# Normalizing the attention probabilities of the second block on GpSimd instead of VectorE

## The chip, the cores and the metric

The kernel runs as one program on 1 core of a Trainium2 chip. TensorE multiplies matrices, VectorE and ScalarE do elementwise work, GpSimd elementwise work from SBUF alone, and SyncE issues most of the loads. The metric is the time of one execution on the device in microseconds (us). Before the change the median of 3 runs is 4014.93 us (4013.55 to 4018.3).

## The reference, cut to what matters

Two blocks of two layers each run one after the other on a sequence of 1024 tokens of width 1024. The change lies in the second block. There each layer projects the tokens (and 256 context tokens), attends, gates, applies a Fourier transform, merges the heads and applies a feed-forward. The attention's softmax has a sink, whose exponential counts in the sum alone:

```python
s_loc = jnp.where(valid[None, :, None, None], s_loc, NEG_INF)
s_ctx = jnp.einsum('bnqhgd,bchd->bnhgqc', qb, ck, ...) * scale
p = jax.nn.softmax(jnp.concatenate([s_loc, s_ctx, s_sink], axis=-1), axis=-1)
out = (jnp.einsum('bnhgqk,bnkhd->bnqhgd', p_loc, vw)
       + jnp.einsum('bnhgqc,bchd->bnqhgd', p_ctx, cv))
```

The context tokens attend to each other in layer 0 only, with the same softmax. All of it is fp32.

## The kernel before, in words

Every product with weights is taken in three parts: the high part of the weights with the high and the low part of the activations, and the low part of the weights with the high part of the activations. Weights come in chunks of 128x1024. SyncE loads a raw chunk into one of four buffers (`wraw` and `late_raw`, two each). ScalarE copies it to the high part `whi` (L1902). GpSimd subtracts this from the raw chunk and writes the low part `wlo`, in two instructions of 128x512 (`split_low`, L1883). `whi` and `wlo` have two buffers, so the subtraction for chunk g+2 waits until chunk g is through on TensorE (`lin_done`) and until ScalarE has written `whi` (`w_hi`). In the second block GpSimd does nothing else. Its program is one loop over chunks.

Attention is spread over the chunks of other work. It has 40 steps in layer 0 (8 tiles of 128 queries times 4 pairs of heads, then 2 context tiles times 4) and 32 in layer 1. Step i belongs to one chunk: steps 0 to 11 to the last projection, 12 and 13 to the Fourier transform over the channels, 14 to 29 to the 16 half chunks of the Fourier transform over the tokens, and the rest to the merge. In the chunk of step i:

- TensorE takes the scores of step i (`score`, L2759 to L2776), some weight products, then the products with the values for step i-2 (`values`, L2797), more weight products, and the transposes of the probabilities of step i-1 in two halves (`turn`, L2739), the second at the end of the chunk.
- VectorE takes the maxima of step i (`maximum`, L2340 to L2350; the last two of its instructions are 128x2 with both inputs in SBUF), copies the first half of the transposes of step i-1 from PSUM to SBUF (`turned`, L2365), normalizes step i (`normalize`: it adds the sink's exponential, L2373, takes the reciprocal, L2374, and multiplies the two halves of the probabilities, 128x640 each, or 128x256 in a context step, by their reciprocals, L2376), does what other work the chunk has, and copies the second half of step i-1.
- ScalarE takes the exponentials of step i (L1976, L1978) and copies the rest of the transposes (L1985).

The other work that VectorE has behind `normalize` is: adding squares for the norms (`add_square`, L2283) in half chunks 7 to 10 of the token transform and in the merges; the low parts of the merged activations (`low`, L2304) in half chunks 14 and 15 and at the end of a merge; in the channel transform the low parts L2463, from PSUM. Ahead of it come scalings (`scale`, L2295) in half chunks 12 to 14, and updates (L2316, L2317). The order of each engine is written out by hand. Queues are in order, and engines wait for one another by semaphores alone. TensorE's `turn` waits for `pn_ready`, counted once per half, and for both copies of the half before. `turned_before` lets the sums of the norms (L2646) and the gate's products (L2834) wait for the copies, since they share PSUM banks. The copy of the transform's result (`transformed`, L2505) frees the banks for the next products.

The first block, which the change doesn't touch, already multiplies its probabilities on GpSimd (L565, 128x1024).

Of the kernel before, what the change touches and what calls it, by code (L numbers as in the profile page):

```python
# [13 lines left out]
ALU = mybir.AluOpType  # L14
# [3 lines left out]
P = 128  # L18
D = 1024
KB = D // P  # L20
# [4 lines left out]
DEPTH = 2  # L25
UNITS = DEPTH * NB
# [66 lines left out]
class Chain:  # L93
# [16 lines left out]
    def link(self, ins):  # L110
        self.n += 1
        ins.then_inc(self.sem, 1)
        value = self.base + self.n
        self.eng.wait_ge(self.sem, value if isinstance(self.reg, int) else self.reg * self.per + value)
# [251 lines left out]
def first_block(nc, t, a, sem):  # L366

    with ExitStack() as ctx:
# [16 lines left out]
        mx, nmax, sink_arg, esum, esink, rden = (sb(n, [P, 2, 4]) for n in ("mx", "nmax", "sink_arg", "esum", "esink", "rden"))  # L385
# [14 lines left out]
        probs = [big[:, 2 * n:2 * n + 2, :].rearrange("p a (g k) -> p (a g) k", k=2 * P) for n in range(2)]  # L400
# [21 lines left out]
        def sig(name, per, start=0):  # L422
            return Sig(sem(name), per, start)
# [18 lines left out]
        r_scores, r_kd, r_qd, r_out, r_evac, r_state = (sig(n, NT) for n in ("r_scores", "r_kd", "r_qd", "r_out", "r_evac", "r_state"))  # L442
        s_ready, nm_ready, exp_done, rden_ready, pn_ready = (sig(n, 8) for n in ("s_ready", "nm_ready", "exp_done", "rden_ready", "pn_ready"))
        pt_done, pt_evac_a, pt_evac_d, pv_done = (sig(n, 8) for n in ("pt_done", "pt_evac_a", "pt_evac_d", "pv_done"))
        t["attention"] = s_ready, nm_ready, exp_done, pt_done, pt_evac_a, pt_evac_d, pv_done
        ao_done = sig("ao_done", NT - 1)
        head_sq_ready, head_summed, head_rstd, head_scaled = (sig(n, 4) for n in ("head_sq_ready", "head_summed", "head_rstd", "head_scaled"))
# [1038 lines left out]
RAW2 = 4  # L1486
# [11 lines left out]
IN_ROWS, MERGE_ROWS, FF_ROWS = [[0, NB, 1], [NB, 0, 1]], [[0, 1, NB], [0, 1]], [[0, NB, 1], [0, 1]]  # L1498

S1_AT, DFT_AT, WO_AT, FF_AT = [], [], [], []  # L1500
# [11 lines left out]
CHUNKS2 = _at  # L1512
# [5 lines left out]
STEPS2 = [LATENT_STEPS + CTX // P * 4, LATENT_STEPS]  # L1518
STEP_AT = [0, STEPS2[0]]
DIM_POINT, DFT_POINT = IN2, IN2 + 2  # L1520
# [5 lines left out]
def second_block(nc, t, a, sems, out):  # L1526

    sem = sems
    with ExitStack() as ctx:
# [17 lines left out]
        nmax, sink_arg, esum, esink, rden = (sb(n, [P, 2, 2]) for n in ("nmax2", "sink_arg2", "esum2", "esink2", "rden2"))  # L1547
# [22 lines left out]
        probs = [staged_flat[:, 2 * KEYS * n:2 * KEYS * (n + 1)].rearrange("p (v k) -> p v k", v=2) for n in range(2)]  # L1570
# [27 lines left out]
        def sig(name, per, start=0):  # L1598
            return Sig(sem("c_" + name), per, start)
# [17 lines left out]
        ctx_dft, ctx_dft_done = sig("ctx_dft", 0), sig("ctx_dft_done", 0)  # L1617
        s_ready, nm_ready, exp_done, pt_done, pt_evac_a, pt_evac_d, pv_done = (Sig(v.sem, 1, 8 * UNITS) for v in t["attention"])
        s_far, pn_ready, ao_done = sig("s_far", 1), sig("pn_ready", 1), sig("ao_done", 1)
        a_sq = sig("a_sq", FF_CH)  # L1620
        a_hi_ready, a_ready = sig("a_hi_ready", FF_CH), sig("a_ready", FF_CH, 2)
        saved = sig("saved", 0)
# [4 lines left out]
        def rows_in(l, order):  # L1627

            return [Rows(l, b) for b in order[l]]
# [86 lines left out]
        def step_of(l, i):  # L1716

            return (i // 4, i % 4) if i < LATENT_STEPS else (SEQ // P + (i - LATENT_STEPS) // 4, (i - LATENT_STEPS) % 4)

        def blocks_of(tile):  # L1720

            return (3, 2) if tile < SEQ // P else (1, 1)
# [70 lines left out]
        def merge_at(l, b):  # L1793
            return WO_AT[l] + MERGE_ROWS[l].index(b) * KB

        def ff_at(l, b):
            return FF_AT[l] + FF_ROWS[l].index(b) * FF2

        def merge_point(l, b, k):

            return MERGE_POINT + MERGE_ROWS[l].index(b) * KB + k
# [73 lines left out]
        @block.gpsimd  # L1875
        def _(pool):
            def split_low(g, r):

                s = r % 2
                pool.wait_ge(*w_hi.after(g, 1))  # L1880
                pool.wait_ge(*lin_done.after(g, -1))
                for half in (slice(0, D // 2), slice(D // 2, D)):
                    last = nc.gpsimd.tensor_tensor(wlo[:, s, half], raw_chunk[r][:, half], whi[:, s, half].bitcast(F32), ALU.subtract)  # L1883
                last.then_inc(*w_split.one)

            with pool.Fori(0, CHUNKS2 // RAW2) as i:
                for n in range(2, RAW2 + 2):
                    split_low(RAW2 * i + n, n % RAW2)
            for g in range(CHUNKS2 // RAW2 * RAW2 + 2, CHUNKS2 + 2):
                split_low(g, g % RAW2)  # L1890

        @block.scalar
        def _(act):
# [376 lines left out]
        def _(dve):  # L2270
            link = dve_chain.link
# [95 lines left out]
            def normalize(l, i):  # L2367

                if i >= STEPS2[l]:
                    return  # L2370
                r, n = i % 2, sum(blocks_of(step_of(l, i)[0])) * P
                dve.wait_ge(*exp_done.after(STEP_AT[l] + i, 1))
                link(nc.vector.tensor_tensor(esum[:, r, :], esum[:, r, :], esink[:, r, :], ALU.add))  # L2373
                link(nc.vector.reciprocal(rden[:, r, :], esum[:, r, :]))  # L2374
                for kv in range(2):
                    nc.vector.tensor_scalar(probs[r][:, kv, 0:n], probs[r][:, kv, 0:n], rden[:, r, kv:kv + 1], None, ALU.mult)\  # L2376
                      .then_inc(*pn_ready.one)

            def project(l, p):
                nxt, attending = next_in(l, p.b), p.b == 1  # L2380
# [816 lines left out]
```

## Time and profile before

| | |
|---|---|
| median of 3 runs | 4014.93 us |
| the profiled execution, its time | 4015.34 us |
| the profiled execution, its span | 4013.6 us |
| TensorE busy | 3716.5 us (93%) |
| VectorE busy | 2118.4 us (53%) |
| ScalarE busy | 1726.9 us (43%) |
| GpSimd busy | 1779.6 us (44%) |
| mean matmul of L2672 with h_hi, h_lo | 0.384 and 0.377 us |
| attention of the second block, layer 0 | from 1390 to 1782 us |
| attention of the second block, layer 1 | from 2890 to 3185 us |

The profile is of one execution; its span leaves out some 2 us at the ends. An engine's busy time is the time in which an instruction runs on it. Matmuls overlap, so their durations are longer than their distance. A wait is read from the idle time in front of an instruction and from who ended it.

### The profile page before, as it was taken

To read this page: it belongs to the slowest core of one execution; us is meant where nothing else is said; L and a number is where in the kernel's file an instruction comes from. 1 tells how busy PE (TensorE), PEld (TensorE's weight loads), DVE (VectorE), ACT (ScalarE), POOL (GpSimd) and SP (SyncE) were. 2 spreads that over 40 slices of the span, in tenths; PEclk is the share of its full clock that TensorE was granted. 3 is DMA by queue.
4 is the path that set the end of the run, shared out by engine and by line. 5 is a ranking of instruction groups with operands and counts; after the bars stand their busy time and mean duration, and the time that the engine had idled before them with its cause. 6 is when DMAs were issued, how large, how long until landed. Compare 5 with 4: busy or idle time off the path is not lost.

```text
span 4013.6 us, 61376 instructions
## 1 busy us (share of the span) xinstructions
PE 3716.5 (93%) x22388; PEld 2993.7 (75%) x22388; DVE 2118.4 (53%) x3355; ACT 1726.9 (43%) x2899; POOL 1779.6 (44%) x1288
## 2 busy tenths in 40 slices
PE   4999999999998899888999999999899899999997
PEld 3767767767766677657888898887777778887886
DVE  5546546546546567667324655236667574235234
ACT  2355355355355544555223454235444553233223
POOL 1543544434443522325455885454322355455444
PEclk7999999999999899998999999999999999999999
DMA  6333433433333321212232453322221223232323
GB/s 252 122 124 125 138 118 126 146 111 134 127 122 109 103 82 48 64 53 87 91 98 92 145 173 110 94 94 79 85 84 53 63 79 94 89 96 96 94 92 103
DMA packets 127222, 421.32 MB, mean 105 GB/s; under 512 B 17281, under 2 KB 19105, under 8 KB 126369
## 3 DMA queue, kind: packets, MB, share of 16 engines
q1 hardware_dynamic: 121488, 410.09, 31.1%
q10 hardware_dynamic: 5520, 8.34, 0.6%
q8 instruction: 140, 2.29, 0.2%
q14 instruction: 74, 0.60, 0.0%
HBM read 397.40 MB, written 6.29 MB: 101 GB/s over the span
## 4 chain that ended last, share of the span: by engine, by line
PE 54%; DVE 7%; ACT 3%; issue 2%; POOL 0%; DMA 0%; SPq 0%; ACTq 0%; DVEq 0%; POOLq 0%
PE lin L2672 30%; PE lin L2681 15%; PE bankO L2797 2%; PE lin L2930 2%; PE bankT L2739 2%; DVE x L2317 1%; DVE tmp L2283 1%; DVE y L2316 1%; PE scores L2772 1%; DVE h_lo L2306 1%; DVE staged L2295 1%; PE lin L2814 1%; ACT whi L1902 0%; PE lin L2702 0%; PE scores L2773 0%
## 5 line engine op out<-in xcount | busy, mean ns | idle before, releaser
L1883 POOL TENSOR_TENSOR wlo<-late_raw,whi 128x512 fp32r<-128x512 f32 x456 | 641.2, 1429 | 764.4 <-PE lin L2681 497.6
L1883 POOL TENSOR_TENSOR wlo<-wraw,whi 128x512 fp32r<-128x512 f32 x452 | 635.9, 1431 | 716.8 <-PE lin L2681 497.5
L2672 PE MATMUL lin<-h_hi,whi 128*128 128x512 f32 (+1 forms) x1896 | 715.2, 384 | 47.4 <-ACT f L2196 12.4
L2672 PE MATMUL lin<-h_lo,whi 128*128 128x512 f32 (+1 forms) x1896 | 701.1, 377 | 0.0
L523 POOL TENSOR_TENSOR wlo<-wraw,whi 128x512 fp32r<-128x512 f32 x260 | 359.5, 1404 | 464.6 <-PE lin L1168 290.2
L2672 PE MATMUL lin<-a_hi,whi 128*128 128x512 f32 (+1 forms) x1280 | 471.9, 376 | 12.0 <-ACT tmp L2205 7.8
L2672 PE MATMUL lin<-a_lo,whi 128*128 128x512 f32 (+1 forms) x1280 | 468.7, 374 | 0.0
L2672 PEld LDWEIGHTS lin<-h_hi,whi 128*128 128x128 f32 x1896 | 368.2, 194 | 133.5 <-issue 24.9
L1902 ACT ACTIVATE whi<-late_raw 128x1024 fp32r<-128x1024 f32 x228 | 239.2, 1057 | 517.2 <-PE lin L2672 414.9
L1902 ACT ACTIVATE whi<-wraw 128x1024 fp32r<-128x1024 f32 x226 | 237.3, 1057 | 497.0 <-PE lin L2672 413.3
L2681 PE MATMUL lin<-h_hi,wlo 128*128 128x512 f32 (+1 forms) x1896 | 439.8, 375 | 1.2 <-POOL wlo L1883 0.8
L2672 PEld LDWEIGHTS lin<-h_lo,whi 128*128 128x128 f32 x1896 | 368.7, 194 | 61.1 <-issue 1.2
L2681 PEld LDWEIGHTS lin<-h_hi,wlo 128*128 128x128 f32 x1896 | 334.0, 190 | 66.6 <-issue 6.2
L2550 DVE TENSOR_TENSOR tmp<-tmp 128x512 f32<-128x512 f32 (+1 forms) x160 | 185.3, 1158 | 335.3 <-ACT tmp L2205 330.2
L1160 PE MATMUL lin<-h_hi,whi 128*128 128x512 f32 x800 | 334.9, 419 | 10.5 <-DVE h_lo L869 10.5
L1160 PE MATMUL lin<-h_lo,whi 128*128 128x512 f32 x800 | 323.4, 404 | 0.0
L2681 PE MATMUL lin<-a_hi,wlo 128*128 128x512 f32 (+1 forms) x1280 | 296.9, 376 | 2.1 <-POOL wlo L1883 2.1
L2672 PEld LDWEIGHTS lin<-a_hi,whi 128*128 128x128 f32 x1280 | 241.9, 189 | 67.2 <-ACT tmp L2205 15.7
L2672 PEld LDWEIGHTS lin<-a_lo,whi 128*128 128x128 f32 x1280 | 242.0, 189 | 46.2 <-issue 0.2
L620 ACT ACTIVATE whi<-wraw 128x1024 fp32r<-128x1024 f32 x130 | 136.7, 1057 | 302.6 <-PE lin L1160 206.6
L2576 DVE TENSOR_TENSOR y<-lin,y 128x512 f32 (+1 forms) x96 | 66.4, 692 | 378.4 <-PE lin L2681 378.2
L2681 PEld LDWEIGHTS lin<-a_hi,wlo 128*128 128x128 f32 x1280 | 226.7, 190 | 51.3 <-POOL wlo L1883 3.4
(381 smaller groups left out, 6435.4 us busy)
## 6 DMA issues: line engine op xcount, KB each, us to landing
wraw<-in_w SPq DMA_DIRECT2D x332, 512.0 KB, 3.5
late_raw<-in_w SPq DMA_DIRECT2D x212, 512.0 KB, 3.5
mod_ring<-in_w_ada SPq DMA_DIRECT2D x96, 512.0 KB, 4.6
mod_ring<-in_w_mod SPq DMA_DIRECT2D x32, 512.0 KB, 4.6
tmp<-tmp SPq DMA_DIRECT2D x224, 64.0 KB, 2.0
first_ring<-in_w_mod SPq DMA_DIRECT2D x16, 512.0 KB, 16.6
wraw<-in_dft_tokens SPq DMA_DIRECT2D x16, 512.0 KB, 3.5
late_raw<-in_dft_tokens SPq DMA_DIRECT2D x16, 512.0 KB, 3.5
```

The lines of the kernel that those rows point to most:

```text
L523: last = nc.gpsimd.tensor_tensor(wlo[:, s, half], wraw[:, s, half], whi[:, s, half].bitcast(F32), ALU.subtract)
L620: nc.scalar.activation(whi[:, s, :], wraw[:, s, :], ACT.Copy).then_inc(*w_hi.one)
L1160: last = nc.tensor.matmul(bank[c % 2], whi[:, c % 2, k * P:(k + 1) * P], h[:, k, :], start=(k == 0 and h is h_hi), stop=False)
L1883: last = nc.gpsimd.tensor_tensor(wlo[:, s, half], raw_chunk[r][:, half], whi[:, s, half].bitcast(F32), ALU.subtract)
L1902: nc.scalar.activation(whi[:, s, 0:D], raw_chunk[r], ACT.Copy).then_inc(*w_hi.one)
L2550: nc.vector.tensor_tensor(tmp[:, 2 + s, 0:w], tmp[:, 4 + s, 0:w], tmp[:, 4 + s, 0:w], ALU.mult).then_inc(*a_sq.one)
L2576: nc.vector.tensor_tensor(part, bank[s][:, 0:p.w], part, ALU.add).then_inc(*lin_free.one)
L2672: last = nc.tensor.matmul(bank[s][:, 0:p.w], whi[:, s, k * P:(k + 1) * P], h[:, k, 0:p.w], start=(k == 0 and h is parts[0]), stop=False)
L2681: last = nc.tensor.matmul(bank[s][:, 0:p.w], wlo[:, s, k * P:(k + 1) * P], parts[0][:, k, 0:p.w], start=False, stop=(k == KB - 1))
L2739: last = nc.tensor.transpose(out, probs[i % 2][:, kv, k * P:(k + 1) * P], ident[:])
L2797: last = nc.tensor.matmul(bankO[half, g * P:(g + 1) * P], v, probsT[:, kv, at:at + P], start=(k == 0), stop=(k == n - 1))
L2930: return nc.tensor.matmul(bank[c][:, 0:2 * P].rearrange("p (t n) -> p t n", t=2), x_part[:, k, cols], w[:, 0:2, k * P:(k + 1) * P], start= ...
```

## The change

VectorE no longer multiplies the probabilities. It adds the sink's exponential and takes the reciprocal, which now raises `sums_ready`, a semaphore of the first block that is used on. Before it writes the reciprocals it waits for the multiplication of two steps before, which reads the same buffer. GpSimd waits for `sums_ready` and multiplies both halves by the reciprocal, broadcast over the columns, and raises `pn_ready`. Since that must come between the subtractions at the right places, GpSimd's program is written out chunk by chunk, except for the feed-forwards, which keep a loop of four chunks each.

```diff
+            def normalize(l, i):
+                if i >= STEPS2[l]:
+                    return
+                r, n = i % 2, sum(blocks_of(step_of(l, i)[0])) * P
+                pool.wait_ge(*sums_ready.after(STEP_AT[l] + i, 1))
+                for kv in range(2):
+                    nc.gpsimd.tensor_tensor(probs[r][:, kv, 0:n], probs[r][:, kv, 0:n], rden[:, r, kv:kv + 1].to_broadcast([P, n]),
+                                            ALU.mult).then_inc(*pn_ready.one)
+            def split_behind(g):
+                split_low(g + 2, (g + 2) % RAW2)
...
+                for h in range(DFT):
+                    normalize(l, DFT_POINT + h)
+                    if h % 2:
+                        for s in range(2):
+                            split_behind(DFT_AT[l] + h - 1 + s)
+                for b in MERGE_ROWS[l]:
+                    for k in range(KB):
+                        normalize(l, merge_point(l, b, k))
+                        split_behind(merge_at(l, b) + k)
...
                 link(nc.vector.tensor_tensor(esum[:, r, :], esum[:, r, :], esink[:, r, :], ALU.add))
-                link(nc.vector.reciprocal(rden[:, r, :], esum[:, r, :]))
-                for kv in range(2):
-                    nc.vector.tensor_scalar(probs[r][:, kv, 0:n], probs[r][:, kv, 0:n], rden[:, r, kv:kv + 1], None, ALU.mult)\
-                      .then_inc(*pn_ready.one)
+                no = STEP_AT[l] + i
+                if no >= 2:
+                    dve.wait_ge(*pn_ready.after(2 * (no - 2), 2))
+                nc.vector.reciprocal(rden[:, r, :], esum[:, r, :]).then_inc(*sums_ready.one)
```

In the projections and the channel transform GpSimd's order is the same: the product of the step, then the subtraction of the chunk two ahead.

GpSimd's program of the second block before is this loop (`wlo` is the low part, `whi` the high part, `wraw` and `late_raw` the raw chunks):

```order
L1883 TENSOR_TENSOR wlo<-late_raw,whi 128x512 x2
L1880 REGISTER_ALU
L1883 TENSOR_TENSOR wlo<-wraw,whi 128x512 x2
L1880 REGISTER_ALU
L1883 TENSOR_TENSOR wlo<-wraw,whi 128x512 x2
L1886 REGISTER_ALU
L1886 COMPARE_AND_BRANCH
```

And this is GpSimd's program now in layer 0, at the end of the token transform and the start of the merge (`staged` holds the probabilities, `rden` the reciprocals):

```order
L1885 TENSOR_TENSOR wlo<-wraw,whi 128x512 x4
L1895 TENSOR_TENSOR staged<-staged,rden 128x640 x4
L1885 TENSOR_TENSOR wlo<-late_raw,whi 128x512 x4
L1895 TENSOR_TENSOR staged<-staged,rden 128x640 x4
L1885 TENSOR_TENSOR wlo<-wraw,whi 128x512 x4
L1895 TENSOR_TENSOR staged<-staged,rden 128x640 x2
L1885 TENSOR_TENSOR wlo<-late_raw,whi 128x512 x2
```

In the transform four multiplications, those of an even and of the following odd half chunk, stand ahead of every four subtractions. In the merge it is two and two.

On VectorE, these are half chunks 13 (its last rows), 14 and 15 of the token transform before, without the rows of the maxima (`h_lo` is the low part of the activations):

```order
L2295 SCALAR_TENSOR_TENSOR f<-f,g_m,tmp 128x512 x2
L2365 COPY staged<-bankT 128x384
L2373 TENSOR_TENSOR esum<-esum,esink 128x2
L2374 RECIPROCAL rden<-esum 128x2
L2376 TENSOR_SCALAR staged<-staged,rden 128x640 x2
L2304 TENSOR_TENSOR h_lo<-q,h_hi 128x512 x4
```

And now:

```order
L2333 SCALAR_TENSOR_TENSOR f<-f,g_m,tmp 128x512 x2
L2403 COPY staged<-bankT 128x384
L2411 TENSOR_TENSOR esum<-esum,esink 128x2
L2415 RECIPROCAL rden<-esum 128x2
L2342 TENSOR_TENSOR h_lo<-q,h_hi 128x512 x4
```

The two multiplications between the reciprocal and the four subtractions are gone from VectorE, and the subtractions stand right behind the reciprocal. TensorE's, ScalarE's and SyncE's instructions keep their order.

## Rows read from the trace of the kernel before

**Rows 1.** The page's part 4, the chain that ended last, shares by engine.

```profile
PE 54%; DVE 7%; ACT 3%; issue 2%; POOL 0%; DMA 0%; SPq 0%; ACTq 0%; DVEq 0%; POOLq 0%
```

**Rows 2.** Two stretches: length, then each engine's busy us; layers 0, 1.

```profile
1392.00:1782.00 390.00, 352.20 (x2404) 277.43 (x2406) 260.65 (x591) 191.04 (x430) 102.81 (x78) 0.97 0.18 58
2892.00:3185.00 293.00, 274.45 (x2038) 223.16 (x2038) 202.26 (x475) 144.09 (x320) 79.67 (x62) 0.98 0.20 63
```

**Rows 3.** One line's instructions, VectorE's multiplication: ns min/median/max.

```profile
L2376 DVE TENSOR_SCALAR staged<-staged,rden x144: 343/551/1646, 1393.6 to 3172.9; 128x640 f32<-128x640 f32 x128, 128x256 f32<-128x256 f32 x16
```

**Rows 4.** The same view of three lines of GpSimd.

```profile
L565 POOL TENSOR_TENSOR big<-big,rden x32: 1892/1893/1897, 227.4 to 1166.0; 128x1024 f32<-128x1024 f32 x32
L538 POOL TENSOR_TENSOR big<-bsum x32: 1031/1069/1489, 101.7 to 1008.3; 128x512 f32<-128x512 f32 x32
L1883 POOL TENSOR_TENSOR wlo<-late_raw,whi x456: 1262/1297/5462, 1251.6 to 3993.0; 128x512 fp32r<-128x512 f32 x152
```

**Rows 5.** Timelines, first merge: start, us, engine, line; in brackets idle before, releaser.

```profile
1679.37 2.97 POOL L1883 TENSOR_TENSOR wlo<-late_raw,whi 128x512 fp32r<-128x512 f32 x2 [7.14 <-PE lin L2681]
1679.38 3.51 DVE L2283 TENSOR_TENSOR tmp<-tmp 128x512 f32<-128x512 f32 x2
...
1683.62 0.29 PE L2797 MATMUL bankO<-staged,vx 128*64 128x128 f32 x1 [1.12 <-DVE staged L2365]
```

**Rows 6.** Timelines, a multiplication and the transposes that read it.

```profile
1631.06 1.01 DVE L2376 TENSOR_SCALAR staged<-staged,rden 128x640 f32<-128x640 f32 x2
...
1635.43 0.71 PE L2739 MATMUL bankT<-ident,staged 128*128 128x128 f32 x5
```

**Rows 7.** Timelines, ahead of the gate's products in the last projection.

```profile
1490.45 3.11 DVE L2376 TENSOR_SCALAR staged<-staged,rden 128x640 f32<-128x640 f32 x2
...
1494.13 1.97 PE L2834 MATMUL bankT<-w_s,y 128*64 128x128 f32 x32 [1.72 <-issue]
```

**Rows 8.** TensorE's timeline, the channel transform.

```profile
1521.62 1.99 PE L2891 MATMUL lin<-dims,f 128*128 128x256 f32 x8 [0.99 <-DVE h_lo L2463]
```

**Rows 9.** Timelines, half chunk 10 of the token transform.

```profile
1609.15 1.02 DVE L2376 TENSOR_SCALAR staged<-staged,rden 128x640 f32<-128x640 f32 x2
1610.08 1.41 DVE L2283 TENSOR_TENSOR tmp<-tmp 128x512 f32<-128x512 f32 x2
...
1612.18 1.95 PE L2646 MATMUL bankT<-tmp,ones 128*128 128x512 f32 x4 [0.98 <-DVE staged L2365]
```

**Rows 10.** Timelines, half chunks 13 to 15 and the first matmuls behind.

```profile
1638.15 2.03 DVE L2376 TENSOR_SCALAR staged<-staged,rden 128x640 f32<-128x640 f32 x2
1638.57 5.24 POOL L1883 TENSOR_TENSOR wlo<-late_raw,whi 128x512 fp32r<-128x512 f32 x4 [10.29 <-ACT whi L1902]
...
1643.94 1.41 DVE L2295 SCALAR_TENSOR_TENSOR f<-f,g_m,tmp 128x512 f32<-128x512 f32 x2
1646.18 0.74 PE L2739 MATMUL bankT<-ident,staged 128*128 128x128 f32 x5 [1.06 <-ACT staged L1985]
1647.17 2.49 DVE L2304 TENSOR_TENSOR h_lo<-q,h_hi 128x512 fp32r<-128x512 f32 x4
1650.27 0.29 PE L2797 MATMUL bankO<-staged,vx 128*64 128x128 f32 x1 [1.06 <-DVE staged L2365]
...
1654.59 1.02 DVE L2376 TENSOR_SCALAR staged<-staged,rden 128x640 f32<-128x640 f32 x2
1658.43 0.69 DVE L2304 TENSOR_TENSOR h_lo<-f,h_hi 128x512 fp32r<-128x512 f32 x1 [1.02 <-ACT h_hi L1958]
1660.25 0.79 PE L2672 MATMUL lin<-h_hi,whi 128*128 128x512 f32 x1 [3.59 <-DVE f L2505]
1660.84 0.63 PE L2672 MATMUL lin<-h_lo,whi 128*128 128x512 f32 x1
```

**Rows 11.** Timelines, four subtractions and the maximum's last instruction.

```profile
1603.17 4.98 POOL L1883 TENSOR_TENSOR wlo<-late_raw,whi 128x512 fp32r<-128x512 f32 x4 [10.89 <-ACT whi L1902]
1605.76 1.17 DVE L2350 TENSOR_TENSOR sink_arg<-nmax,neg_sink 128x2 f32<-128x2 f32 x1
```

More of the change, by code:

```diff
@@ L444, in first_block @@
         pt_done, pt_evac_a, pt_evac_d, pv_done = (sig(n, 8) for n in ("pt_done", "pt_evac_a", "pt_evac_d", "pv_done"))
+        t["sums_ready"] = rden_ready
         t["attention"] = s_ready, nm_ready, exp_done, pt_done, pt_evac_a, pt_evac_d, pv_done
@@ L1619, in second_block @@
         s_far, pn_ready, ao_done = sig("s_far", 1), sig("pn_ready", 1), sig("ao_done", 1)
+        sums_ready = Sig(t["sums_ready"].sem, 1, 8 * UNITS)
         a_sq = sig("a_sq", FF_CH)
@@ L1884, in split_low, with feed_forward @@
                 last.then_inc(*w_split.one)
[L1886 to L1890, printed above, removed]
+            def normalize(l, i):
[8 more added lines that the diff above has]
+                split_low(g + 2, (g + 2) % RAW2)
+            def feed_forward(l, b):
+                g = ff_at(l, b)
+                with pool.Fori(0, FF2 // RAW2) as i:
+                    for n in range(RAW2):
+                        split_low(RAW2 * i + (g + n + 2), (g + n + 2) % RAW2)
+            for l in range(DEPTH):
+                for p in rows_in(l, IN_ROWS):
+                    for s in range(2 if l and p.context else IN2):
+                        if p.b == 1:
+                            normalize(l, s)
+                        if s != GV2:
+                            for c in (GV2, s) if s == GV2 + 1 else (s,):
+                                split_behind(p.in_at + c)
+                for half in range(2):
+                    normalize(l, DIM_POINT + half)
+                for h in range(DFT):
[7 more added lines that the diff above has]
+                        split_behind(merge_at(l, b) + k)
+                for b in FF_ROWS[l]:
+                    feed_forward(l, b)
         @block.scalar
@@ L2370, in normalize @@
                     return
-                r, n = i % 2, sum(blocks_of(step_of(l, i)[0])) * P
+                r = i % 2
                 dve.wait_ge(*exp_done.after(STEP_AT[l] + i, 1))
                 link(nc.vector.tensor_tensor(esum[:, r, :], esum[:, r, :], esink[:, r, :], ALU.add))
-                link(nc.vector.reciprocal(rden[:, r, :], esum[:, r, :]))
-                for kv in range(2):
-                    nc.vector.tensor_scalar(probs[r][:, kv, 0:n], probs[r][:, kv, 0:n], rden[:, r, kv:kv + 1], None, ALU.mult)\
-                      .then_inc(*pn_ready.one)
+                no = STEP_AT[l] + i
+                if no >= 2:
+                    dve.wait_ge(*pn_ready.after(2 * (no - 2), 2))
+                nc.vector.reciprocal(rden[:, r, :], esum[:, r, :]).then_inc(*sums_ready.one)
             def project(l, p):
```

## The prediction

> **What bounds the kernel now.** I read the chain of waits first, to see which engine the end hangs on. It names TensorE for 54% of the span and VectorE for 7%, and GpSimd for nothing [rows 1]. So work may move to GpSimd for nothing unless TensorE ends up waiting for it, or for an engine that it slows. The change touches only the second block's attention steps, so next I read the busy times in the two stretches in which they run. In 390 us (layer 0) TensorE is busy 352.20, and in 293 us (layer 1) 274.45 [rows 2]. That leaves 56 us in which anything can be gained. GpSimd is busy 102.81 and 79.67 us there, about a quarter, so it has room by its sum. The last view was the timeline, place by place: at each wait of TensorE I looked for what VectorE and GpSimd did just before it.
>
> **What is removed and what is added.** Removed from VectorE are 144 multiplications, with a median of 0.551 us [rows 3], some 79 us in all. The trace has no row for the operation added, GpSimd's multiplication of 128x640 by a broadcast column. The nearest rows are GpSimd instructions with a broadcast operand: 1.069 us for 512 columns and 1.893 for 1024 [rows 4]. The line between 1.031 (the shortest of the first) and 1.893 gives 1.68 ns for a column, so about 1.25 us for 640 columns and 0.6 for the 256 of a context step. From below it is bounded by the row for 512, 1.07. From above it is bounded by the subtraction that makes the low weights, whose shortest is 1.262 for 512 [rows 4], which is 1.58 for 640. I take 1.25, so 2.5 us for a step, and 128 x 1.25 + 16 x 0.6 = 170 us in all.
>
> The Trainium skill ("GPSIMD Engine Reference", section "3.1 Elementwise") gives about 2.6 cycles for each element at 1.2 GHz for a tensor_tensor, an estimate of 1.39 us for 640 columns, where my rows give 1.25. By it the sum below would be about 2 us larger.
>
> **Is the product late for TensorE?** No. Of the 72 steps the tightest I found has its two multiplications on VectorE at 1631.06 for 1.01 us, and the first transpose that reads them at 1635.43 [rows 6]. GpSimd has the first half ready after 1.3 us instead of 0.6 and the second after 2.6 instead of 1.0. That is 1.6 us later at most, against over 3 us of slack. Behind the multiplication on GpSimd's queue stand the next weights' subtractions. They move by up to 2.5 us and are read a chunk or two later (5 to 10 us), so neither TensorE nor ScalarE's next copy nor the load of raw weights waits for them. VectorE's new wait, for the product of two steps before, has been met for a whole step. SyncE's queue isn't touched. The loops written out cost an entry of a loop per feed-forward, which GpSimd's idle time covers.
>
> **What the engines do to one another.** This is where the sum comes from. At 1679.37 GpSimd starts two subtractions and at 1679.38 VectorE two additions with both inputs in SBUF. The additions take 3.51 us, where the same pair alone takes 1.41, and the subtractions 2.97 [rows 5, 9]. The two engines take turns: VectorE's instruction waits for the end of GpSimd's and GpSimd's next one for VectorE's. One such VectorE instruction then costs about 1.75 us instead of 0.70. With a GpSimd multiplication of 1.25 I take 1.72. Reads of PSUM (the copies behind the transposes) don't do that. The Trainium skill ("GPSIMD Engine Reference", section "1. Specifications") says that the engines share SBUF interfaces and contend when VectorE's instruction has two SBUF inputs or is in a two-port mode. It speaks against this change, and the trace agrees, with 3.51 against 1.41. So wherever VectorE has such instructions right behind the reciprocal, and TensorE waits for what follows them, the move takes 1.0 us away and puts one turn of GpSimd before each of the next two.
>
> **Gains.** At 1490.45 the two multiplications, 1.02 us elsewhere, take 3.11 beside a subtraction, and TensorE waits 1.72, which nothing but the copy behind them explains [rows 7]. They go, and with them 1.7 us, in layer 0 alone. In the Fourier transform over channels VectorE's subtractions come earlier, which takes 0.6 off the wait of 0.99 [rows 8], and 0.3 in layer 1. In the merge, ahead of TensorE's wait of 1.12 at 1683.62, the chain from the reciprocal's end to the copy is 1.02 + 3.51, about 4.6 us [rows 5, 9]. Two turns make 0.1 + 2 x 1.72, about 3.6, so 1.0 off that wait, again in layer 0 only, where the subtractions fall beside both additions. Sum: -3.6.
>
> **Losses with instructions behind.** All in the token transform (16 half chunks, counted from 0) and twice, once a layer.
> - Half chunk 10: from the start of the multiplications (1609.15) over the two additions and the copy to TensorE at 1612.18, which has waited 0.98, is 3.03 us [rows 9]. After: 0.1 + 2 x 1.72 + 0.6 for the copy = 4.15. +1.1, twice 2.3 with rounding.
> - Half chunk 13: the multiplications (2.03, stalled) go, but the four subtractions of 5.24 us that start at 1638.57 now start at about 1640.7, behind the product. The two small instructions of the next maximum and the two scalings (1.41, free) now all wait their turns (boundaries at 1643.2, 1644.5 and 1645.8, the last scaling free), so the copy behind them ends at 1647.7. TensorE, which waits there already (1.06), goes on at 1648.0 instead of 1646.18 [rows 10]. +1.8, twice 3.6.
> - Half chunk 14: 1.02 + 2.49 for four subtractions become 0.1 + 2 x 1.72 + 1.25. TensorE waits 1.06 for the copy behind [rows 10]. +1.3, twice 2.6.
> - Half chunk 15: from the multiplications' start (1654.59, [rows 10]) to the end of the last of four subtractions (1658.43 + 0.69) are 4.5 us. In turns with the product and then with the next weights they take 4 x 1.72 + 0.1 = 7.0. TensorE waits 3.59 for what follows [rows 10]. +2.4 with 0.1 for the slack of the last, twice 4.8.
> - Half chunk 7 has one addition behind: +0.2, twice 0.4. In the merge with context tokens the product is short (0.6) and two places move by about a microsecond with either sign: I take +0.6.
>
> Sum: +14.3.
>
> **Losses by a shift.** In each odd half chunk the four subtractions start behind the product, some 1 us later than at 1603.17 [rows 11], and so end later. The next maximum's last instruction (1605.76, 1.17 us instead of 0.16, [rows 11]) waits for the second boundary after it. Moved over the boundaries that is +0.4 in three half chunks of each layer, and +1.0 in the one shown: +3.4, where TensorE's transposes have waits already. By luck of the phase this term could as well be -3.
>
> The sum is -3.6 + 14.3 + 3.4 = +14.1. On the profiled execution's own 4015.34 that is 4029.4. The median of the runs shown, 4014.93, is 0.4 lower, so I forecast 4029.
>
> **Rivals.**
> - The relief decides (faster). VectorE's next instruction follows the reciprocal on its own engine and may get the interface before the product starts 0.1 us later, or may find it free between two products. Then each of the 8 listed places gives 1.0 back instead, -8, with the gains -3.6: 4003. It decides from the point where VectorE's first instruction behind the reciprocal has its input ready at that moment. Against it: those inputs come from ScalarE, some 0.4 us behind the reciprocal, and the rows show the turns as soon as both are active [rows 5].
> - It cancels (no change). TensorE's waits at these places end by ScalarE or by a table load as often as by VectorE, so half of the losses pass and the shift comes out at zero: -3.6 + 7.2, about 4018.5. For it: the wait at 1646.18 is put down to ScalarE [rows 10].
> - Longer waits also cost clock. Behind the wait of 3.59 at 1660.25 the matmuls take 0.63 us [rows 10] where the mean of that line is 0.38 (in the table of the profile). The trace grants the lower of 1.2 and 2.4 GHz there. Eight such matmuls cost 2 us. If four of the longer waits bring that on, +8, and products of 1.58 instead of 1.25 add 2 x 0.33 at 8 places, +5: about 4042.
> - The change doesn't do what it says, in that GpSimd's product is hidden and VectorE's was too: the time stays. This is in the second case.
>
> **How the numbers follow.** Forecast (4023 to 4036) 0.42, clock and longer products 0.18, cancelled 0.27, relief 0.13. About 0.2%, 8 us, is what a measurement of this kernel can tell from no change. So faster (under 4007) 0.13, same 0.27, slower 0.60. The range is 4006 to 4044: it leaves a tenth on each side and takes in both bounds of the product. The likeliest case alone is 4023 to 4036.
>
> **What will show it.** In the changed profile: GpSimd's product at about 1.25 us, 144 times, and GpSimd's busy time up by 170 us; no wait of TensorE or ScalarE put down to it; VectorE's h_lo subtractions in half chunks 14 and 15 at about 1.7 us instead of 0.62; the waits at 1494 gone, and those at 1612, 1646, 1650 and 1660 longer by 1 to 2.5 us. TensorE's busy time stays and its idle time in the stretches grows by 14. Subtractions that stay at 0.7 us right beside a product would prove me wrong, and so would TensorE waiting for the product itself.

## The result and the profile after

| | before | after |
|---|---|---|
| median of 8 runs | 4013.69 us | 4026.41 us |
| lowest to highest | 4013.26 to 4018.52 | 4024.59 to 4030.43 |
| profiled execution, time | 4015.34 us | 4024.59 us |
| profiled execution, span | 4013.6 us | 4022.5 us |

The ratio is 1.0033 (95% interval 1.0023 to 1.0042): slower by 12.7 us between the medians, where +14.1 was forecast. The profiled execution is the fastest of its eight and shows +9.3. One execution of the second series of the changed kernel (below) was a slow run (6042.14 us) and is left out of its ratio.

First the chain of waits, then the two attention stretches (answering to [rows 2], with limits moved so that they hold the same work; columns as there) and GpSimd's new instruction (ns min/median/max):

```profile
PE 54%; DVE 8%; ACT 3%; issue 1%; POOL 0%; DMA 0%; SPq 0%; ACTq 0%; DVEq 0%; POOLq 0%
...
1392.00:1785.90 393.90, 354.04 (x2407) 277.63 (x2409) 237.82 (x511) 190.73 (x430) 197.22 (x158) 0.96 0.18 58
2896.00:3192.60 296.60, 273.14 (x2038) 221.68 (x2038) 183.28 (x411) 143.78 (x320) 160.96 (x126) 0.98 0.20 62
...
L1895 POOL TENSOR_TENSOR staged<-staged,rden x144: 612/1253/1702, 1393.5 to 3181.3; 128x640 f32<-128x640 f32 x128, 128x256 f32<-128x256 f32 x16
```

The stretches are 3.9 and 3.6 us longer. GpSimd's busy time has nearly doubled in them (over the whole kernel it is up by 178 us, where 170 were forecast), VectorE's has fallen by 23 and 19 us, and the chain still names GpSimd for nothing. The product's median is 1.253 us, the value that the prediction took from the line between 512 and 1024 columns.

Now the places of [rows 7 to 11] (start, us, engine, line; idle before and its releaser in brackets). The gate, the channel transform and half chunk 10:

```profile
1489.77 2.46 POOL L1895 TENSOR_TENSOR staged<-staged,rden 128x640 f32<-128x640 f32 x2 [5.09 <-DVE rden L2415]
1492.08 1.97 PE L2872 MATMUL bankT<-w_s,y 128*64 128x128 f32 x32
...
1519.03 1.99 PE L2929 MATMUL lin<-dims,f 128*128 128x256 f32 x8 [0.43 <-DVE h_lo L2501]
...
1604.97 1.22 DVE L2388 TENSOR_TENSOR sink_arg<-nmax,neg_sink 128x2 f32<-128x2 f32 x1
1608.45 2.91 POOL L1895 TENSOR_TENSOR staged<-staged,rden 128x640 f32<-128x640 f32 x2 [1.03 <-DVE rden L2415]
1608.80 3.10 DVE L2321 TENSOR_TENSOR tmp<-tmp 128x512 f32<-128x512 f32 x2 [0.43 <-ACT tmp L1951]
1612.60 3.52 PE L2684 MATMUL bankT<-tmp,ones 128*128 128x512 f32 x4 [2.14 <-DVE staged L2403]
```

The wait of 1.72 at the gate is gone, and the 0.99 of the channel transform is 0.43. In half chunk 10 the two additions take 3.10 us instead of 1.41, and TensorE waits 2.14 instead of 0.98. The four matmuls behind it, 1.95 us in [rows 9], take 3.52: TensorE is at the lower of its two levels there (granted clock 0.73 in the 6.2 us from 1612.4, below).

Half chunks 12 to 15 and the first matmul behind:

```profile
1632.48 2.46 POOL L1895 TENSOR_TENSOR staged<-staged,rden 128x640 f32<-128x640 f32 x2 [2.82 <-DVE rden L2415]
1642.01 4.98 POOL L1885 TENSOR_TENSOR wlo<-late_raw,whi 128x512 fp32r<-128x512 f32 x4
1645.70 2.49 DVE L2333 SCALAR_TENSOR_TENSOR f<-f,g_m,tmp 128x512 f32<-128x512 f32 x2
1647.04 1.21 PE L2968 MATMUL lin<-wlo,h_hi 128*128 128x256 f32 x8 [1.46 <-POOL wlo L1885]
1648.81 0.74 PE L2777 MATMUL bankT<-ident,staged 128*128 128x128 f32 x5 [0.56 <-DVE staged L2403]
1648.85 4.59 DVE L2342 TENSOR_TENSOR h_lo<-q,h_hi 128x512 fp32r<-128x512 f32 x4
1649.43 1.74 DVE L2342 TENSOR_TENSOR h_lo<-q,h_hi 128x512 fp32r<-128x512 f32 x1
1654.05 0.29 PE L2835 MATMUL bankO<-staged,vx 128*64 128x128 f32 x1 [2.22 <-DVE staged L2403]
...
1658.41 2.91 POOL L1895 TENSOR_TENSOR staged<-staged,rden 128x640 f32<-128x640 f32 x2 [6.13 <-DVE rden L2415]
1658.77 3.11 DVE L2342 TENSOR_TENSOR h_lo<-u,h_hi 128x512 fp32r<-128x512 f32 x2 [0.43 <-ACT h_hi L1996]
1661.80 3.42 DVE L2342 TENSOR_TENSOR h_lo<-f,h_hi 128x512 fp32r<-128x512 f32 x2
1666.33 0.80 PE L2710 MATMUL lin<-h_hi,whi 128*128 128x512 f32 x1 [5.90 <-DVE f L2543]
```

In half chunk 14 four subtractions take 4.59 us instead of 2.49. The first had begun before GpSimd's product and the last began behind it, so only the middle two pay: the line at 1649.43 is the second of the four by itself, 1.74 us, against 0.69 for one in [rows 10]. In half chunk 15 all four pay. The first two (3.11 together) take turns with the product, the last two (3.42 together, 1.7 each) with the next weights' subtractions, which stand right behind the product in GpSimd's queue. TensorE then waits 5.90 instead of 3.59.

TensorE runs the same instructions around the token transform in every kernel, so the transform can be measured by itself: from its first matmul (1529.33 us before) to the first matmul of the merge (1660.25 before, 1666.33 after). Worked out so from every trace, in us, beside the median time and the ratio to the kernel before in the same session (95% interval; the medians of before were 4015.40 beside the first four experiments, 4015.51 beside the next four, 4015.33 and at last 4016.72):

```
kernel                                     layer 0  layer 1   median    ratio
before, first profile                       130.92   132.20   4013.69
before, second profile (below)              130.91   132.13   4013.75   0.9993 (0.9983 to 1.0003)
after, first profile                        139.59   138.65   4026.41   1.0033 (1.0023 to 1.0042)
after, second profile                       139.55   140.41   4026.25   1.0027 (1.0016 to 1.0038)
order alone, no product on GpSimd           130.68   131.92   4011.45   0.9990 (0.9981 to 0.9999)
order alone, again                          131.89   131.89   4008.47   0.9986 (0.9977 to 0.9996)
product on GpSimd in 4 half chunks only     138.91   138.89   4026.57   1.0030 (1.0019 to 1.0040)
... in all but these 4                      132.74   132.77   4010.00   0.9984 (0.9975 to 0.9993)
... in all but these 4, again               132.77   132.80   4008.36   0.9985 (0.9976 to 0.9994)
... outside the token transform             131.92   131.89   4009.31   0.9986 (0.9977 to 0.9995)
... in 6 steps expected to gain             130.67   131.93   4013.41   0.9993 (0.9984 to 1.0002)
after, in pieces of 320 columns             136.96   136.94   4018.18   1.0008 (0.9999 to 1.0016)
after, 1280 columns in one instruction      143.89   144.70   4043.21   1.0067 (1.0054 to 1.0079)
after, product behind VectorE's work        133.27   132.68   4012.41   0.9992 (0.9983 to 1.0001)
```

The two transforms together are 15.1 us longer in the first profile after, and 16.8 in the second.

### The profile page after: what moved, and what is told of

Read it like the earlier page. It is cut to its first block, busy times and chain, and to the rows that moved or that the text cites. A ratio compares the mean times of both kernels' runs of the same rounds, so it can differ in the third digit from the quotient of the medians.

```text
span 4022.5 us, 61252 instructions
## 1 busy us (share of the span) xinstructions
PE 3715.4 (92%) x22388; PEld 2990.1 (74%) x22388; DVE 2077.8 (52%) x3211; ACT 1726.7 (43%) x2899; POOL 1957.2 (49%) x1432
## 4 chain that ended last, share of the span: by engine, by line
PE 54%; DVE 8%; ACT 3%; issue 1%; POOL 0%; DMA 0%; SPq 0%; ACTq 0%; DVEq 0%; POOLq 0%
PE lin L2710 30%; PE lin L2719 15%; PE bankO L2835 2%; PE bankT L2777 1%; PE lin L2968 1%; DVE tmp L2321 1%; PE lin L2852 1%; DVE x L2355 1%; DVE staged L2333 1%; DVE h_lo L2342 1%; DVE h_lo L2344 1%; PE scores L2810 1%; DVE y L2354 1%; PE bankT L2684 1%; ACT staged L2014 0%
## 5 line engine op out<-in xcount | busy, mean ns | idle before, releaser
L1895 POOL TENSOR_TENSOR staged<-staged,rden 128x640 f32<-128x640 f32 (+1 forms) x144 | 176.0, 1243 | 334.0 <-DVE rden L2415 334.0
```

Source lines behind the costliest of these rows:

```text
L1895: nc.gpsimd.tensor_tensor(probs[r][:, kv, 0:n], probs[r][:, kv, 0:n], rden[:, r, kv:kv + 1].to_broadcast([P, n]), ALU.mult).then_inc(*pn_r ...
```

## The experiments

Theory A is the prediction's: VectorE and GpSimd take turns, instruction by instruction, in half chunks 10, 13, 14 and 15. Theory B: every moved product costs a little. Theory C: the written-out program costs. Each kernel is the changed one with an edit.

**Which steps.** One condition on both engines decides where a step's product is made (each kernel has one of the five returns; `...` stands for what is left out):

```diff
+def on_gpsimd(l, i):
+    h = i - DFT_POINT
+    return False                      # order alone
+    return h in (10, 13, 14, 15)      # four half chunks
+    return h not in (10, 13, 14, 15)  # the rest
+    return not 0 <= h < DFT           # outside the token transform (run later)
+    return (l, i) in ((0, 10), (0, 31)) or i in (DIM_POINT, DIM_POINT + 1)  # six steps
...
+                if not on_gpsimd(l, i):
+                    ...
+                    dve.wait_ge(*sums_ready.after(no, 1))
+                    if no:
+                        dve.wait_ge(*pn_ready.after(2 * (no - 1), 2))
+                    for kv in range(2):
+                        nc.vector.tensor_scalar(...)
```

Order alone.

> GpSimd's program is written out per chunk as in the change, but VectorE keeps all 144 multiplications. Theory A (the time is lost where VectorE and GpSimd take turns): no change, 4013.7 us within 3. Rival C (the written-out program costs, by its loop entries or its code): about half or more of the 12.7 us, over 4019.

Four half chunks.

> GpSimd multiplies only in half chunks 10, 13, 14 and 15 of the token transform (8 of 72 steps), VectorE in all others. Theory A: these eight steps carry nearly the whole loss, +13.3 by the sum of the prediction, so about 4027. Rival B (every step loses a little, 12.7 / 72 = 0.18 us each): +1.4, about 4015. In the trace by A: the wait of TensorE at the end of the transform near 5.9 us instead of 3.59, the one ahead of the sums of the norms near 2.1 instead of 0.98.

The rest.

> The complement: GpSimd multiplies in the other 64 steps, VectorE in half chunks 10, 13, 14 and 15. Theory A: the gains -3.6, the shift +3.4, half chunk 7 and the context steps +1.0, together +0.8, so about 4014.5. Rival B (a loss spread evenly over the steps): 64 x 0.18 = +11.3, about 4025.

Six steps.

> GpSimd multiplies only in the step beside the gate of the last projection of layer 0, in the two steps of the channel transform of each layer, and in the step of the first merge at 1679 us of layer 0 (6 steps). Theory A: only the gains are left, -3.6, so about 4010. Rival B: 6 x 0.18 = +1.1, about 4015. In the trace by A: the wait of 1.72 at the gate is gone.

Order alone came out at 4011.45, within what was expected, so theory C falls. Four half chunks cost all of it, 4026.57, with the change's waits:

```profile
1613.92 3.65 PE L2699 MATMUL bankT<-tmp,ones 128*128 128x512 f32 x4 [2.13 <-DVE staged L2410]
1655.50 0.29 PE L2850 MATMUL bankO<-staged,vx 128*64 128x128 f32 x1 [2.23 <-DVE staged L2410]
1667.78 0.79 PE L2725 MATMUL lin<-h_hi,whi 128*128 128x512 f32 x1 [5.91 <-DVE f L2558]
```

The rest, 64 of 72 products on GpSimd, came out at 4010.00, 4.5 us under what was expected: theory B falls too. The wait at the end of the transform is back:

```profile
1664.83 0.50 PE L2725 MATMUL lin<-h_hi,whi 128*128 128x512 f32 x1 [3.60 <-DVE f L2558]
```

The fourth kernel missed its forecast: 4013.41 instead of 4010, and no faster than order alone, which moves nothing. The intervals of the two overlap, so this alone decides little. The trace of order alone says more: most of the gains come without the move. At the gate and in the first merge, with every product on VectorE:

```profile
1492.79 2.03 DVE L2428 TENSOR_SCALAR staged<-staged,rden 128x640 f32<-128x640 f32 x2
1492.88 3.06 POOL L1889 TENSOR_TENSOR wlo<-wraw,whi 128x512 fp32r<-128x512 f32 x2 [7.14 <-PE lin L2733]
1495.39 1.86 PE L2886 MATMUL bankT<-w_s,y 128*64 128x128 f32 x30 [0.64 <-issue]
...
1680.41 2.38 DVE L2327 TENSOR_TENSOR tmp<-tmp 128x512 f32<-128x512 f32 x2
1680.46 3.48 POOL L1889 TENSOR_TENSOR wlo<-late_raw,whi 128x512 fp32r<-128x512 f32 x2 [7.14 <-PE lin L2733]
1683.54 0.29 PE L2849 MATMUL bankO<-staged,vx 128*64 128x128 f32 x1
```

Where GpSimd started 0.01 us ahead of VectorE in the merge [rows 5], VectorE now starts 0.05 us ahead and gets one addition through. The pair takes 2.38 us instead of 3.51, and TensorE doesn't wait. At the gate the wait is 0.64 instead of 1.72, with the product still on VectorE.

**How long a turn is.** The same work in instructions of another size, and the same kernel again beside them:

```diff
                 for kv in range(2):
-                    nc.gpsimd.tensor_tensor(probs[r][:, kv, 0:n], ..., ALU.mult).then_inc(*pn_ready.one)
+                    for at in (0, n // 2):
+                        part = probs[r][:, kv, at:at + n // 2]
+                        ins = nc.gpsimd.tensor_tensor(part, part, rden[:, r, kv:kv + 1].to_broadcast([P, n // 2]), ALU.mult)
+                    ins.then_inc(*pn_ready.one)
```

```diff
-                for kv in range(2):
-                    nc.gpsimd.tensor_tensor(probs[r][:, kv, 0:n], ..., ALU.mult).then_inc(*pn_ready.one)
+                both = probs[r][:, :, 0:n]
+                nc.gpsimd.tensor_tensor(both, both, rden[:, r, :].rearrange("p (v o) -> p v o", o=1).to_broadcast([P, 2, n]),
+                                        ALU.mult).then_inc(pn_ready.sem, 2)
```

The change again.

> The changed kernel itself once more, with a second profile, on the chip of the three kernels below. All theories: 12.7 us over the kernel before. By the clock's part of theory A the second profile shows again the wait of 2.14 us ahead of the sums of the norms; whether the matmuls behind it run at the lower clock decides part of the spread between executions.

Pieces.

> As the change, but GpSimd multiplies each half in two instructions of 320 columns, four a step. Theory A (VectorE's instruction waits for the end of GpSimd's current one): a turn shrinks from 1.74 us (1.25 + 0.45) to about 1.16 (0.71 + 0.45), so in half chunk 10 two turns give 1.1 back, in 14 two give 0.5 (two more of its subtractions now fall beside pieces), in 15 two to three give 1.2: -2.8 a layer, about -5.6 against the changed kernel, so 8 rather than 13 us over before. Rival D (the two engines share a rate, and the same bytes cost the same in any pieces): no change, 12.7 over before, and the subtractions stay at 1.7.

One instruction.

> As the change, but one instruction of GpSimd multiplies both halves (128 x 1280, about 2.5 us). Theory A: one VectorE instruction waits for all of it, 3.0 us instead of 1.74, and in half chunk 15 the three behind take turns with the next weights: +0.1 in half chunk 10, +0.4 in 14, +1.3 in 15, about +3.6 for both layers, 16 us over before. Rival D: no change, 12.7 over before.

The change again gave 4026.25, 1.0027. In its layer 1 the four matmuls ahead of the norms ran at the lower level, in the first profile at the higher, after waits of the same length (first profile, then second):

```profile
3109.19 1.96 PE L2684 MATMUL bankT<-tmp,ones 128*128 128x512 f32 x4 [2.14 <-DVE staged L2403]
```

```profile
3107.72 3.50 PE L2684 MATMUL bankT<-tmp,ones 128*128 128x512 f32 x4 [2.13 <-DVE staged L2403]
```

That costs 1.5 us, of which the next wait gives back 0.5, so it is about half of the 1.8 us by which its second transform is longer. Pieces came out at 4018.18: 8.1 us under the change, where theory A expected 5.6, and 2.7 over before, where it expected 8. The direction is theory A's; in the transforms alone the pieces are 4.3 and 6.1 us shorter than the two profiles of the change. The product and half chunk 15:

```profile
L1903 POOL TENSOR_TENSOR staged<-staged,rden x288: 398/720/1169, 1393.9 to 3175.3; 128x320 f32<-128x320 f32 x128, 128x128 f32<-128x128 f32 x16
...
1658.67 2.04 DVE L2350 TENSOR_TENSOR h_lo<-u,h_hi 128x512 fp32r<-128x512 f32 x2 [0.43 <-ACT h_hi L2004]
1660.64 1.20 DVE L2350 TENSOR_TENSOR h_lo<-f,h_hi 128x512 fp32r<-128x512 f32 x1
1664.08 0.80 PE L2726 MATMUL lin<-h_hi,whi 128*128 128x512 f32 x1 [3.75 <-DVE f L2559]
```

A subtraction beside pieces takes 1.20 us (1.16 expected) and the end's wait is 3.75. One instruction for both halves came out at 4043.21, 27.7 over before, where 16 was expected. The mechanism shows, for an addition waits for all of it (half chunk 8), and so does half chunk 15:

```profile
L1901 POOL TENSOR_TENSOR staged<-staged,rden x72: 1039/2320/2623, 1396.6 to 3200.5; 128x1280 f32<-128x1280 f32 x64, 128x512 f32<-128x512 f32 x8
...
1598.26 2.38 DVE L2327 TENSOR_TENSOR tmp<-tmp 128x512 f32<-128x512 f32 x1 [0.63 <-ACT tmp L1957]
1665.27 4.26 DVE L2348 TENSOR_TENSOR h_lo<-u,h_hi 128x512 fp32r<-128x512 f32 x2 [0.43 <-ACT h_hi L2002]
1673.97 0.79 PE L2724 MATMUL lin<-h_hi,whi 128*128 128x512 f32 x1 [7.04 <-DVE f L2557]
```

What was left out were the single additions of half chunks 7 to 9: with short products they lose 0.25 us each (0.93 instead of 0.68), here 1.7, and TensorE has new waits of about 1 us there. The transforms account for 25.5 of the 27.7 (13.0 and 12.5). By rival D, a shared rate, neither kernel should have moved; it falls. The Trainium skill ("GPSIMD Engine Reference", section "1. Specifications") says that the two engines contend for shared interfaces; these runs agree, and show that VectorE waits for the end of a whole instruction of GpSimd's (1.20, 1.74 or 2.4 to 2.8 us for the same work of VectorE's, beside instructions of 0.72, 1.25 and 2.32 us).

**Without the collision.** All products on GpSimd, but begun when VectorE's additions or subtractions are done:

```diff
                 pool.wait_ge(*sums_ready.after(STEP_AT[l] + i, 1))
+                h, sig, first = i - DFT_POINT, norms["mix"], mix(l, 0)
+                if h == 10:
+                    pool.wait_ge(*sig["add"].after(first.no, adds_before("mix", MIX_SQUARES[7]) + 1))
+                if h in (14, 15):
+                    pool.wait_ge(*sig["ready"].after(first.no, 4 * h - 52))
```

> As the change, all products on GpSimd, but in half chunks 10, 14 and 15 GpSimd begins them only when VectorE's additions or subtractions of that half chunk are done, so that no turn is left there but those with the weights. Theory A: the losses of these half chunks go, 1.1 + 1.3 + about 1.6 of the 2.4 (weights still collide in 15), twice, and the clock lost behind the wait ahead of the norms: 8 to 10 us under the changed kernel, 3 to 5 over before. Rival B (the loss is spread, or is that of a product that is late): no gain, or more loss, since the products come 1.4 to 4 us later still.

It came out at 4012.41, 13.8 us under the change, where 8 to 10 were expected, and no slower than before (0.9992). Half chunks 10, 14 and 15:

```profile
1613.61 1.96 PE L2703 MATMUL bankT<-tmp,ones 128*128 128x512 f32 x4 [0.44 <-DVE staged L2414]
1648.88 2.48 DVE L2353 TENSOR_TENSOR h_lo<-q,h_hi 128x512 fp32r<-128x512 f32 x4
1651.50 2.46 POOL L1906 TENSOR_TENSOR staged<-staged,rden 128x640 f32<-128x640 f32 x2 [4.49 <-DVE h_lo L2353]
1657.41 1.29 DVE L2353 TENSOR_TENSOR h_lo<-u,h_hi 128x512 fp32r<-128x512 f32 x2 [0.43 <-ACT h_hi L2007]
1662.66 0.80 PE L2729 MATMUL lin<-h_hi,whi 128*128 128x512 f32 x1 [3.26 <-DVE f L2562]
```

The four subtractions take 2.48 us again, although the product that they used to meet is as long as ever. The transforms are back within 2.9 us of before, though the products come some 2 to 5 us later. So a late product was not the cause, and the overlap was. More came back than expected because in half chunk 15 the next weights' subtractions, which stand behind the product in GpSimd's queue, came out of VectorE's way as well: its last subtraction there takes 0.69 us, where 1.7 was expected to stay. Half chunk 13 was left as it was, and TensorE still waits 1.45 us in it.

**Is any of it faster than before?** Four kernels had come out up to 0.16% under it. So the rest and order alone were run again, beside one with VectorE's product in all 16 half chunks, and at last the kernel before against itself.

> GpSimd multiplies in the projections, the channel transform and the merges; VectorE in all 16 half chunks of the token transform. The shift in the odd half chunks (measured in the traces as about +1.8 us in layer 0 and +0.7 in layer 1 where GpSimd multiplies there) is gone as well, and the gain of 0.6 in the channel transform stays. Theory A: some 2 us under the kernel with the four half chunks alone on VectorE, and some 3 to 6 under before, at about 4009. Rival (GpSimd's products outside the transform gain nothing, and the kernels differ by the program's form or by chance alone): equal to the order-only kernel within its interval.

> The kernel with only half chunks 10, 13, 14 and 15 on VectorE once more, beside the one above and the one below. If its first result (0.9984) was not chance, it comes out 4 to 6 us under before again.

> The kernel with GpSimd's program written out and every product on VectorE once more. Theory A, with the stalls that only one profiled execution of before shows taken as chance: no change against before (0.9985 to 1.0005), and slower than the two above by 2 to 4 us.

> The kernel before itself, profiled again and timed like the others, to tell apart two reasons for the 0.10 to 0.14% of the order-only kernel. Theory F (the form of GpSimd's program moves its subtractions by some hundredths of a microsecond, so that VectorE's instruction starts first at the gate and in the first merge): the second profile of before shows again the multiplications of about 3 us at the gate and the two additions of 3.5 us in the first merge, and the ratio is 1.0000. Rival G (one execution's chance, or the comparison's own error): the stalls are gone in this profile, or the ratio itself strays from 1 by 0.1% or more.

Beside one another they gave 4009.31, 4008.36 and 4008.47: the product on GpSimd in 40 or 64 steps, or in none, is the same time. Two expectations missed: order alone was to be 2 to 4 us slower than the other two, and the kernel without products in the transform 2 us faster than the one with twelve half chunks of them. The transform is 0.9 us a layer shorter without products in it, but that doesn't show in the whole.

The kernel before against itself gave 0.9993 (0.9983 to 1.0003), so 0.07% of a ratio means nothing here. The two ratios of order alone, 0.9990 and 0.9986, have intervals that end just under 1. Over the four sessions the mean of its 22 executions is 4010.5 us, and that of the 111 of the kernel before 4015.0. So the written-out program probably gives some 4 us, 0.1%; of these the traces account for 1.0, in the first merge, and the rest is open. The second profile of before settles half of the question about the stalls:

```profile
1490.42 2.03 DVE L2376 TENSOR_SCALAR staged<-staged,rden 128x640 f32<-128x640 f32 x2
1490.82 2.75 POOL L1883 TENSOR_TENSOR wlo<-wraw,whi 128x512 fp32r<-128x512 f32 x2 [7.21 <-PE lin L2681]
1493.02 1.97 PE L2834 MATMUL bankT<-w_s,y 128*64 128x128 f32 x32 [0.42 <-issue]
...
1678.98 3.50 DVE L2283 TENSOR_TENSOR tmp<-tmp 128x512 f32<-128x512 f32 x2
1683.22 0.29 PE L2797 MATMUL bankO<-staged,vx 128*64 128x128 f32 x1 [1.12 <-DVE staged L2365]
```

At the gate GpSimd starts 0.40 us behind VectorE here (in the first profile 0.03, and there the first multiplication already had to wait) and one multiplication goes through ahead of it: TensorE waits 0.42, not 1.72. That stall was one execution's chance. The merge's is there again to the hundredth, so it belongs to the loop's form of the program. The traces show how: there the subtraction waits for a matmul, and in the loop it begins 0.082 us after the end of that matmul in both profiles, but 0.147 in both profiles of order alone. These 0.065 us let VectorE be first. What in the loop makes GpSimd faster wasn't examined.

## Why the prediction was right, and where it was not

- **Turns of 1.72 us.** Right: 1.74 for each of the two subtractions of half chunk 14 that meet the product, and 3.42 for the two of half chunk 15 that meet the next weights' subtractions.
- **The product is not late.** Right. Two waits of TensorE of 0.56 us (at 1623.74 and 3119.36) are put down to it, but two of 0.56 at the same places were put down to VectorE's multiplication before, so they cost nothing new.
- **Half chunk 10, +1.1.** From the product's start at 1608.45 to TensorE at 1612.60 are 4.15 us, the forecast's number, against 3.03 before.
- **Half chunk 13, +1.8.** It was 1.2: the step begins 1.42 us later than in [rows 6] (1632.48 against 1631.06), and the transposes at 1648.81 come 2.63 later than in [rows 10]. The cause was named only in part. The subtractions of the weights start at 1642.01, so TensorE waits 1.46 for their result itself, which the prediction had excluded ("neither TensorE nor ScalarE's next copy", it said), and the copy behind the scalings is then waited for only 0.56. This is not a turn but GpSimd's queue: TensorE waits for what stands behind the product.
- **Half chunk 14, +1.3.** It was 1.2: TensorE at 1654.05 is 3.78 later than before, 1.15 more than at the end of half chunk 13. Part of the rival of relief showed here, for VectorE's first subtraction did start ahead of the product, but the two behind it paid.
- **Half chunk 15, +2.4.** From the multiplications' or the product's start to the first matmul behind were 5.66 us, and now 7.92: +2.3.
- **The shift, +3.4.** The kernel with all but the four half chunks on GpSimd is longer than order alone by 2.1 and 0.9 us in the transforms, +2.9, or +1.8 by the second pair. The difference between the pairs is a wait of about 1 us ahead of half chunk 10 in layer 0, the one that the prediction counted as +1.0: the second profile of order alone has it too, without any product on GpSimd. Right in sign, too large.
- **All terms in the transforms.** Forecast 13.7 + 3.4 = 17.1 (13.3 of the four half chunks and 0.4 of half chunk 7); measured 15.1 and 16.8. The four half chunks alone are 5.8 in each layer, 11.6 against 13.3, and 9.2 of these are turns. The lower clock, which the sum left out, makes up for part of what the terms overstate.
- **The gains, -3.6.** The waits at the gate, in the channel transform and in the first merge went as forecast, but only in part by moving the product. The channel transform's 0.56 us came from it, in layer 0 alone: the wait is 0.99 in all five traces with VectorE's product there and 0.43 in all nine with GpSimd's. The merge's 1.0 came from writing the program out. Of the gate's 1.7 about 0.4 to 0.6 came from the move: with VectorE's product the wait is 1.72, 0.42, 0.64, 0.60 and 0.00 us in five traces, with GpSimd's 0.00 in all nine. The step that failed is "which nothing but the copy behind them explains": the copy did, but what stalled it was a start of GpSimd 0.4 us early, in one profile.
- **The form of the program, cost nothing.** Order alone stands 4 to 7 us under before by its medians, of which before against itself shows 3.0 as well. Against order alone the change costs more than against before: by the ratios (1.0033 against 0.9990, 1.0027 against 0.9986) some 16 to 17 us, and that is the price of moving the product.
- **The clock's rival, 0.18.** It was true in part: behind the wait of 2.14 us the lower level came in layer 0 of both profiles and in layer 1 of one, at 1.5 us each time, of which the next wait gave back 0.5 to 0.6. It came in both layers of the kernel with four half chunks too, but not behind the 2.33 us in layer 0 of the one with long instructions. Elsewhere it goes either way from one execution to the next:

```profile
1612.40:1618.60 6.20, 5.90 (x32) 3.54 (x32) 2.94 (x9) 3.79 (x8) 0.00 (x0) 0.73 0.00 0
2896.00:2904.00 8.00, 6.77 (x34) 5.47 (x35) 4.70 (x10) 3.94 (x10) 4.97 (x4) 1.00 0.00 0
```

```profile
2892.00:2900.00 8.00, 6.73 (x20) 5.00 (x21) 3.58 (x11) 4.40 (x12) 2.78 (x2) 0.57 0.00 0
```

These are windows of after, then of before at the start of layer 1's attention (the clock is the third number from the end): before lay at 0.57 there and after at 1.00, before steps that take the same in both otherwise, and after gained back some 2 us (by the start times of the same instructions on either side). This is part of why its profile shows +9.3 where the medians show +12.7.

The total was thus right mainly for the reason given, the turns: with the product moved in four half chunks alone the whole loss is there, and without the overlap it is gone. That the number came so close is partly luck. The transforms lost 15.1 and 16.8 us with the lower clock, where 17.1 were forecast without it; the move gained about 1 us elsewhere instead of 3.6; and the written-out program, which was put at nothing, seems to take some 4 us off.

## What to carry to other kernels

Before work goes to an idle GpSimd, look at what VectorE does in the microseconds right behind. Here its instructions with two SBUF inputs waited for the end of GpSimd's current one unless they had started first. So did the multiplication that was moved, which has only one large input; this is the first of the two at the gate before, 1.65 us instead of 0.55:

```profile
1490.45 1.65 DVE L2376 TENSOR_SCALAR staged<-staged,rden 128x640 f32<-128x640 f32 x1
```

Its copies from PSUM took 0.56 us beside the product as elsewhere. So the price is the number of such instructions on the path times nearly the length of GpSimd's (1.05 us each for 1.25), less what VectorE is rid of, whatever the busy shares say. Look also at what stands behind the moved work in GpSimd's own queue, as in half chunk 13. If the work must go there, start it behind that of VectorE (a wait more, 13.8 us less here), or cut it into shorter instructions (8 us less). And a stall that hangs on which of two engines starts first by some tenths of a microsecond is booked as a gain only if a second profile of the kernel before shows it too. A change that also rewrites an engine's program needs a run of the rewriting alone.

## What was not expected of the hardware

- GpSimd's multiplication by a broadcast column took 0.720 us for 320 columns, 1.253 for 640 and 2.320 for 1280, which is 0.19 + 1.67 ns for each column, while its subtraction of 512 columns with fp32r output took 1.262 at least. So one long instruction saves 0.19 us of GpSimd's time and cost this kernel 17 us.
- A start 0.01 us earlier or 0.05 us later decides whether two additions take 3.50 or 2.38 us.
- How soon GpSimd's subtraction starts hangs on its place in the loop. For the chunks in `late_raw`, the first two of the four in the loop's body, it began 0.082 us after the matmul that it waited for, or 0.158 after ScalarE's copy. For the other two, and for all four in the written-out program, these were 0.147 and 0.078.
